# The taps of a 31-wide depthwise convolution move their running sum from SBUF to a PSUM bank, one channel tile at a time

## What is computed

```
glu = c_v * sigmoid(c_g)
yc, conf_hist = causal_dwconv(glu, hist['conf'], p['conf_dw_w'])      # width 31, 512 channels
o_c = silu(layernorm(yc + p['conf_dw_b'], p['conf_ln_g'], p['conf_ln_b']))
```

## Time and profile before

| | before |
|---|---|
| time, median of 3 runs | 1775.3 us (1775.08 to 1779.56) |
| the profiled execution: time, span | 1775.84 us, 1773.0 us |
| TensorE (PE) busy | 1512.1 us, 85% |
| VectorE (DVE) busy | 918.6 us, 52% |
| ScalarE (ACT) busy | 581.3 us, 33% |
| GpSimd (POOL) busy | 557.2 us, 31% |
| TensorE's granted clock, mean | 0.910 |

### The profile page before, as it was taken

The page is one execution under the profiler, slowest core; times in us unless marked ns, Lnnn a source line. Parts: engine busy times, 40 slices in busy tenths (PEclk is TensorE's granted clock), DMA queues, the critical chain, the costliest instruction groups (busy, mean ns, idle before and its releaser), DMA issues. The chain is left out here.

```text
span 1773.0 us, 28178 instructions
## 1 busy us (share of the span) xinstructions
PE 1512.1 (85%) x11047; PEld 1396.2 (79%) x11047; DVE 918.6 (52%) x1286; ACT 581.3 (33%) x918; POOL 557.2 (31%) x310
## 2 busy tenths in 40 slices
PE   4886878688897988799888889888676999999995
PEld 3886877688897988776656659888566999999995
DVE  5159896889968675433233332264335555552112
ACT  3322560212133223433221232444324334433222
POOL 2255545343342333011111014310412444343440
PEclk9898996899998999899888879999877999999998
DMA  7144523433342444267544426433322333332331
GB/s 220 48 111 121 144 74 89 126 105 107 105 146 84 143 113 136 56 193 223 145 129 125 137 74 198 126 95 107 114 66 66 90 96 96 89 91 79 91 99 49
DMA packets 254643, 199.83 MB, mean 113 GB/s; under 512 B 15780, under 2 KB 212957, under 8 KB 254104
## 3 DMA queue, kind: packets, MB, share of 16 engines
q1 hardware_dynamic: 234149, 169.47, 33.1%
q10 hardware_dynamic: 19371, 23.86, 4.1%
q0 software_dynamic: 992, 4.72, 0.8%
HBM read 187.89 MB, written 10.81 MB: 112 GB/s over the span
## 5 line engine op out<-in xcount | busy, mean ns | idle before, releaser
L822 PE MATMUL pb<-xh,wh 128*128 128x260 f32 x2176 | 650.7, 299 | 51.7 <-DVE xl L1555 22.6
L822 PE MATMUL pb<-xl,wh 128*128 128x260 f32 x2176 | 634.2, 291 | 0.0
L822 PE MATMUL pb<-xh,rawl 128*128 128x260 f32 x2176 | 632.5, 291 | 0.0
L776 POOL TENSOR_TENSOR rawl<-raw,wh 128x1024 fp32r<-128x1024 f32 (+2 forms) x152 | 339.4, 2233 | 909.5 <-ACT wh L1169 908.7
L822 PEld LDWEIGHTS pb<-xh,wh 128*128 128x128 f32 x2176 | 431.4, 198 | 66.5 <-issue 44.3
L822 PEld LDWEIGHTS pb<-xl,wh 128*128 128x128 f32 x2176 | 431.8, 198 | 0.7
L822 PEld LDWEIGHTS pb<-xh,rawl 128*128 128x128 f32 x2176 | 430.4, 198 | 0.0
L1169 ACT ACTIVATE wh<-raw 128x1024 fp32r<-128x1024 f32 (+2 forms) x208 | 201.6, 969 | 545.0 <-PE pb L822 493.4
L822 PE MATMUL sd<-ar 128*128 128x128 f32 (+7 forms) x1488 | 262.7, 389 | 95.6 <-DVE ar L1555 62.3
L822 PEld LDWEIGHTS sd<-ar 128*128 128x128 f32 (+4 forms) x1488 | 178.9, 193 | 141.0 <-issue 75.8
L791 POOL TENSOR_TENSOR ar<-ar 128x512 f32<-128x512 f32 x128 | 189.0, 1476 | 248.9 <-DMA ar<-in_cache_fox_k 226.1
(11 more groups left out here) (174 smaller groups left out, 1685.8 us busy)
## 6 DMA issues: line engine op xcount, KB each, us to landing
raw<-in_w_in SPq DMA_DIRECT2D x80, 512.0 KB, 4.2
ar<-in_cache_fox_k SPq DMA_DIRECT2D x128, 256.0 KB, 2.8
ar<-in_cache_fox_v SPq DMA_DIRECT2D x128, 256.0 KB, 3.0
raw<-in_w_ffn_in SPq DMA_DIRECT2D x44, 512.0 KB, 3.9
raw<-in_w_branch SPq DMA_DIRECT2D x32, 256.0 KB, 3.1
raw<-in_w_ffn_out SPq DMA_DIRECT2D x16, 512.0 KB, 3.9
ar<-in_cache_mem_k ACTq DMA_DIRECT2D x1, 4096.0 KB, 19.1
raw<-in_w_out SPq DMA_DIRECT2D x8, 512.0 KB, 3.9
```

The source lines that it names most:

```text
L776: pool.tensor_tensor(rawl[:, p % RING, 0:kt, :], raw[:, p % RING, 0:kt, :], wh[:, p % (AHEAD + 1), 0:kt, :].bitcast(F32), SUB).then_inc(lo ...
L822: return pe.matmul(o, l, r, start=start, stop=stop, skip_group_check=True)
```

## The change

The running sum of a tap moves from `oC` in SBUF to `s3`, one PSUM bank of 512 fp32 columns; only the last of the 31 taps writes to `oC`. As there is one such bank, the four channel tiles come one after the other, and each tap waits for the tap right before it. Tap 0 is cut in two: 512 columns to `s3`, the 8 sample columns to `oC`. After each half piece the taps stand half before and half behind the K page. As `s3` is taken now, the sums of the length norms (`l2p`) move from four quarter banks of 260 columns to two banks of 512 and, for the last 8 columns of each, to `s2`; ScalarE reads them with two instructions in place of one.

```
-TAPS = [(j, c) for pair in range(2) for j in range(CFW) for c in (2 * pair, 2 * pair + 1)]
+TAPS = [(j, c) for c in range(KB) for j in range(CFW)]
...
-            background("tap", {"cv": 4, "cg": 4, "gx": h, "ac": 2 - h, "ah": 2 - h, "ab": 2 - h}.get(kind, 2))
+            n_tap = {"cv": 4, "cg": 4, "gx": h, "ac": 2 - h, "ah": 2 - h, "ab": 2 - h}.get(kind, 2)
+            background("tap", n_tap - n_tap // 2)
             background("k", h if kind == "gx" else 1 + (p % 8 == 0))
+            background("tap", n_tap // 2)
...
-                            last = mm(sd[:, 2 * j + h, 0:TH], ones, lsq2[:, j, h * TH:(h + 1) * TH])
+                            last = mm(sd[:, j, :], ones, lsq2[:, j, 0:SEQ]) if h == 0 else \
+                                mm(s2[:, NB * j:NB * j + NB], ones, lsq2[:, j, SEQ:T])
...
-                        fn(lrs2[:, :, :].rearrange("p j (h c) -> p (j h) c", h=2), sd[:, :, 0:TH], ACT.Ln, bias=eps6[:, 0:1])
+                        fn(lrs2[:, :, 0:SEQ], sd[:, 0:2, :], ACT.Ln, bias=eps6[:, 0:1])
+                        fn(lrs2[:, :, SEQ:T], s2[:, 0:2 * NB].rearrange("p (j b) -> p j b", j=2), ACT.Ln, bias=eps6[:, 0:1])
...
                 if j == 0:
-                    own(dve.tensor_scalar(oC[:, c, :], g[:, 30:30 + T], w[:, 30:31], col(V_CB + c), MUL, ADD))
+                    if c == 0:
+                        dve.wait_ge(pe_s.sem, upto(pe_works, ITEMS.index(("sm", 3))))
+                    else:
+                        dve.wait_ge(dve_c.sem, tap_at[c - 1])
+                    dve_c.by(dve.tensor_scalar(s3, g[:, 30:30 + SEQ], w[:, 30:31], col(V_CB + c), MUL, ADD))
+                    tap_at[c] = dve_c.n
+                    dve_c.by(dve.tensor_scalar(oC[:, c, SEQ:T], g[:, 30 + SEQ:30 + T], w[:, 30:31], col(V_CB + c), MUL, ADD))
...
-                if c in tap_at:
-                    dve.wait_ge(dve_c.sem, tap_at[c])
-                dve_c.by(dve.scalar_tensor_tensor(out=oC[:, c, 0:SEQ], in0=g[:, j - 1:j - 1 + SEQ], scalar=w[:, j - 1:j],
-                                                  in1=oC[:, c, 0:SEQ], op0=MUL, op1=ADD))
+                dve.wait_ge(dve_c.sem, tap_at[c])
+                dve_c.by(dve.scalar_tensor_tensor(out=oC[:, c, 0:SEQ] if j == CFW - 1 else s3, in0=g[:, j - 1:j - 1 + SEQ],
+                                                  scalar=w[:, j - 1:j], in1=s3, op0=MUL, op1=ADD))
                 tap_at[c] = dve_c.n
```

## The result

The changed kernel takes **1749.4 us** (median of 4 runs, 1745.2 to 1756.4) beside 1775.2 for the kernel before on the same chip: a ratio of 0.9855, 95% interval 0.9815 to 0.9894, so 1.5% faster, with an interval wholly below 1. The forecast was 1750, with faster at 0.81. The execution profiled after took 1745.22 us, the fastest of the four, with a span of 1743.4 and a mean granted clock of 0.919 in place of 0.910. So the two profiles lie 30.6 us apart and the medians 26.

The account below looks back on a forecast made before the run. TensorE's 74.5 us of idle time in the tap stages, 121 to 505 us, bound the gain, but for the clock. Savings of 11.4 + 3.9 + 8.0 + 2.7 = 26.0 us off 1775.8 gave 1750 us, range 1730 to 1772.

Parts of the forecast that it names:

- A: Stage from 121 to 175 us, weight pieces of cv, cg and first gx: 11.4 us saved, all on the path.
- B: Stage to 335 us, gx with length norms, then the sample tokens' delta rule: 3.9 us saved.
- C: Stage from 335 to 505 us, the prompt's delta rule: 8.0 us saved.
- 2.7 of clock: First tap stage: with shorter idle times TensorE's mean granted clock rises from 0.83 to 0.90, giving 2.7 us.
- Hidden, at nothing: Effects counted as costing or giving no time, among them the sums of pages coming half a step earlier.
- A tap at 0.69 us: VectorE: a tap with its sum in PSUM takes 0.69 us, by the row with a PSUM input.
- The norms' 2.8: Length norms, second tap stage: four steps at 0.7 us each for extra matmuls and ScalarE's second logarithm, 2.8 us lost.
- the 6.7 of VectorE's saving: Second tap stage: of 14.7 us saved on VectorE, 6.7 lie on the path, before the length norms' cost.
- Another wait takes the place: Rival: VectorE comes to wait for pages, GpSimd's products or halves of weights instead; 1771 us, chance 0.13.
- the same in the other stages left out: Clock gain in the tap stages after the first: not counted in the forecast.
- under 9 us: Sign of being right: TensorE's waits for VectorE in the prompt's delta rule fall below 9 us from 16.6.
- more than the sum: Rival: less blocked GpSimd frees pages sooner and the clock recovers in all stages; 39 us saved, 1737 us, chance 0.20.

Follow-up runs that it names:

- the second: Another profiled execution of the changed kernel, nothing altered, from its rerun beside the kernel before: 1746.8 us.

## Why the prediction was right, and where its steps were not

- *What bounds the kernel, and the mechanism:* right. The taps lost time to GpSimd, and the bank takes them out of its way: with GpSimd thinned the two kernels are 2.3 us apart, and the order alone gains nothing. All the taps together save 36 us of VectorE (37.6 forecast).
- *The number, 1750 us:* 1749.4, and so close in part by luck. The profile after, of the fastest run, lost 30.6 us: 13.0 in A (14.1 forecast with its clock), 1.0 in B (3.9), 11.0 in C (8.0) and 5 outside the three, where nothing was forecast. What was forecast too high in A and B offsets C, and the 5 us outside offset the 4 by which the typical run is longer than that one.
- *A, 11.4 us and 2.7 of clock:* 11.2 and 1.8 in the first profile, 11.7 and 2.4 in the second. The sum is right, but not all of its reasons. "Hidden, at nothing", said of the sums of pages half a step earlier, failed: without alternating A took 0.5 to 4 us more, and the whole kernel 6 to 14. How much of A's 13.0 us the shorter taps would have given without the earlier sums is known no better than that.
- *A tap at 0.69 us:* mis-sized, 0.75. The row taken as the nearest differs from a tap in two things, PSUM and the scalar, and I put its 0.06 us down to PSUM. The runs show that they belong to the column of weights. A group of the kernel before that has a column and both inputs in SBUF, 24 operations over 520 columns at 0.758 us, could have told the two apart. A tap's start to the next instruction's is 0.66 us, or 0.79 if that is a tap (four in 3.12 us, against 2.73 with no wait between neighbours), where I had 0.60 and 0.72. It hardly mattered: 7 us less of VectorE left the time where it was.
- *The Trainium skill's fixed costs* ("VectorE: DVE Perf Modes", TRN2 errata): it gives 120 cycles for a PSUM source and 58 for an SBUF source, and by an estimate from these a tap would have become 65 ns longer undisturbed. The thinned pair shows 0.754 us with the sum in SBUF and 0.752 in PSUM, and a tap that reads PSUM and writes SBUF takes 0.744; the measurement decides, as the prediction had it. But the row it rested on (0.694 against 0.750) showed the scalar's price and not PSUM's, and the 0.745 us from which its estimate starts stands in no row (the median is 0.750).
- *B, 3.9 us:* mis-sized, 1.0, and none in the second profile. The norms' 2.8 is not contradicted (2 us alone, with an interval from nothing to 5). What failed is the 6.7 of VectorE's saving: it counted the taps' collisions as gone, but operations that now stand beside GpSimd's are stretched in their place, 3 us in the step shown above, in both profiles. TensorE's named waits for VectorE in B did fall, from 15.0 to 8.7 us; its wait behind that step rose by 2.7 and that for ScalarE by 1.9. "Another wait takes the place" was right for this stage alone.
- *C, 8.0 us:* 11.0 and 8.6 in the two profiles, of which 5.2 and 5.1 are idle time and 5.8 and 3.5 TensorE's own work at a clock of 0.95 and 0.94 in place of 0.91. The saving on the path was put too high, and "the same in the other stages left out" left out a term that made up for it. So the sign "under 9 us" of TensorE's waits for VectorE missed (12.0 and 13.4).
- The rival "more than the sum" was half there: its clock came in C, and not in B, where the granted clock was 0.86 (0.87 before). GpSimd's halves stayed as they were, as forecast (2.44 and 2.43 us in the mean of 120), but its products of pages went from 1.48 to 1.40 us, 9 us over 128; what these gave isn't told apart.

## What to carry to other kernels

In this kernel a tap with both inputs in SBUF pays for what GpSimd does beside it (1.085 us in the mean of 120, 0.754 with GpSimd thinned), and a running sum in PSUM takes it out of that (0.752); to know what is to be gained, thin GpSimd's work in both kernels and see whether the difference goes. A row that prices an operation should differ from it in one thing only: here a scalar column passed for the price of a place. And once the stretched operations are gone from a stage, its schedule was tuned for what no longer holds, so the number of taps in a piece was worth trying again (1736.9 us, a further gain that is likely and not shown).

## What the runs showed of the hardware that was not expected

- A column of 128 weights in place of a number costs VectorE's operation over 512 columns 0.06 us (0.752 and 0.691); a tap that reads and writes one PSUM bank takes no longer than one in SBUF (0.752 and 0.754), and one that writes to PSUM instead of SBUF 0.008 longer. Tap 0, with one input, does pay for it (0.81 and 0.55).
- GpSimd stretched small operations most in proportion: a product over 32 columns took 2.20 us in place of 0.19, and four copies with a single input from SBUF 1.90 in place of 0.86. With GpSimd thinned the changed kernel has 0.31 and 0.87 there. The sums of pages were not stretched: a mean of 0.680 us over 128 beside the same GpSimd, and 0.680 with GpSimd thinned.
- The new order and alternating together gave nothing without the bank (1.0003); with the bank alternating is worth 6 to 14 us by two runs: two changes on one chain didn't add up.
